# One more step of the decoder kernel: all expert rows summed on TensorE, and the expert ring worked two rows at a time

## The reference

```python
eidx = ...                      # 8 heads x 16 experts per token, by product keys and two top-16
g = jax.nn.softmax(fs, axis=-1)
u = u_tab[eidx]                 # (token, head, k, 1024)
v = v_tab[eidx]
a = jax.nn.gelu(jnp.einsum('pd,phkd->phk', xb, u), approximate=False)
return jnp.einsum('phk,phkd->pd', g * a, v)
```

## Time and profile before

| what | value |
|---|---|
| time, median of 3 runs | 2869.25 us (2858.16 to 2870.89) |
| profiled execution: span from first to last instruction | 2849.4 us |
| its own time beside the span | not listed; the three timed runs lie 9 to 21 us above this span |
| TensorE matmul busy | 1959.6 us, 69% |
| VectorE busy | 1637.4 us, 57% |
| ScalarE busy | 397.6 us, 14% |
| GpSimd busy | 652.7 us, 23% |
| mean granted TensorE clock | 0.786 of full speed |
| HBM traffic over the span | 240 GB/s |

### The profile page before, as it was taken

One profiled execution on the slowest core, in us unless ns is written; L12 is line 12 of the kernel. 1 busy time (PEld: TensorE's weight loads), 2 busy tenths in 40 slices (PEclk: granted clock), 3 DMA queues, 4 the chain that ended last, 5 costly groups with the idle time before them and its releaser, 6 DMA issues.

```text
span 2849.4 us, 19084 instructions
## 1 busy us (share of the span) xinstructions
PE 1959.6 (69%) x6466; PEld 1073.8 (38%) x6466; DVE 1637.4 (57%) x3431; ACT 397.6 (14%) x993; POOL 652.7 (23%) x585
## 2 busy tenths in 40 slices
PE   7997789997786522677777776775666676852334
PEld 4433556695486411333233333332233232631110
DVE  3303733302369887565666666655765666477766
ACT  1101123211011100111111011101121111010010
POOL 0000000000000213343344343332433342232232
PEclk9998755556997766789889888997888887676677
DMA  3214160003000457899989999896988889885586
GB/s 109 89 74 34 5 212 1 1 1 158 34 1 1 173 207 321 363 382 363 372 345 357 378 373 360 329 372 261 365 345 317 339 330 403 351 354 236 236 332 266
DMA packets 114049, 680.20 MB, mean 239 GB/s; under 512 B 28768, under 2 KB 32544, under 8 KB 36448
## 3 DMA queue, kind: packets, MB, share of 16 engines
q0 software_dynamic: 83168, 604.55, 53.6%
q1 hardware_dynamic: 30784, 74.44, 8.1%
HBM read 672.55 MB, written 10.55 MB: 240 GB/s over the span
## 4 chain that ended last, share of the span: by engine, by line
PE 35%; DMA 21%; DVE 19%; POOL 7%; issue 5%; ACT 2%; POOLq 0%; DVEq 0%; ACTq 0%
PE bank L696 31%; DMA arena<-in_uv,arena 21%; POOL arena L677 7%; DVE arena L1635 4%; PE bank L708 3%; DVE arena L1430 3%; DVE arena L1427 2%; PE bank L1733 2%; DVE arena L1432 1%; ACT arena L1309 1%; DVE arena L1652 1%; DVE arena L1472 1%; DVE arena L1473 1%; DVE arena L1469 1%; ACT arena L1107 1%
## 5 line engine op out<-in xcount | busy, mean ns | idle before, releaser
L696 PE MATMUL bank<-arena 128*128 128x512 f32 (+13 forms) x4672 | 1513.1, 487 | 783.6 <-ACT arena L1309 658.4
L696 PEld LDWEIGHTS bank<-arena 128*128 128x128 f32 (+4 forms) x4672 | 809.4, 224 | 1423.3 <-ACT arena L1309 703.3
L677 POOL DMA_INDIRECT arena<-in_uv,arena x544 | 616.7, 1134 | 1671.2 <-PE bank L696 1537.7
L1635 DVE CUSTOM_DVE_ANT_0 arena<-arena 128x1024 f32<-128x1024 f32 x544 | 655.4, 1225 | 440.2 <-DMA arena<-in_uv,arena 436.5
L1652 DVE SCALAR_TENSOR_TENSOR arena<-arena 128x1024 f32<-128x1024 f32 x267 | 343.2, 1285 | 9.5
L1733 PE MATMUL bank<-arena 128*128 128x512 f32 (+13 forms) x972 | 312.0, 481 | 46.1 <-DVE arena L2086 15.3
L1733 PEld LDWEIGHTS bank<-arena 128*128 128x128 f32 (+3 forms) x972 | 157.9, 197 | 199.6 <-issue 160.9
L708 PE MATMUL bank<-arena 128*128 128x128 f32 (+3 forms) x716 | 141.5, 342 | 36.1 <-DVE arena L1395 11.8
L1304 ACT ACTIVATE arena<-arena 128x4 f32<-128x4 f32 x136 | 27.7, 204 | 881.6 <-DVE arena L1635 877.6
L1107 ACT ACTIVATE arena<-bank 128x512 f32<-128x512 f32 (+6 forms) x229 | 112.3, 517 | 231.4 <-PE bank L708 209.0
L708 PEld LDWEIGHTS bank<-arena 128*128 128x128 f32 (+3 forms) x716 | 97.2, 172 | 122.2 <-issue 73.5
(11 more groups left out here) (219 smaller groups left out, 683.4 us busy)
## 6 DMA issues: line engine op xcount, KB each, us to landing
arena<-in_w_pq SPq DMA_DIRECT2D x8, 2048.0 KB, 12.8
arena<-in_w_in SPq DMA_DIRECT2D x6, 2048.0 KB, 7.6
arena<-in_uv,arena POOLq DMA_INDIRECT x544, 11.0
arena<-in_w SPq DMA_DIRECT2D x4, 2048.0 KB, 13.8
arena<-in_w_out SPq DMA_DIRECT2D x4, 2048.0 KB
arena<-in_xT SPq DMA_DIRECT2D x1, 2176.0 KB, 8.5
arena<-in_C SPq DMA_DIRECT2D x1, 2064.0 KB, 10.3
out_s_C<-arena SPq DMA_DIRECT2D x1, 2064.0 KB
```

Of the source, the lines that this page charges most:

```text
L677: nc.gpsimd.indirect_dma_start(uv[r], None, i["uv"], bass.IndirectOffsetOnAxis(eidx_u[:, t, s0 + r:s0 + r + 1], 0))\
L696: return te.matmul(out, l, r, start=start, stop=stop)
L1635: last = ve.tensor_tensor_reduce(out=uv[r][:, 0:D], in0=uv[r][:, 0:D], in1=x_sb[:, t, :], scale=1.0, scalar=0.0, op0=ALU.mult, op1=ALU.add ...
```

## The change

All eight rows of an iteration go through the diagonal matmul on TensorE. `acc_v`, its additions on VectorE, the matmul with the identity at a tile's end and the counters `s_vf` and `s_y` are gone. Dots, gelu, gate product, diagonals and the release of ring places go by pairs of rows instead of halves of four: VectorE makes two dots, then waits for the gelu of that pair and multiplies two gates; `s_free` counts four times an iteration, and GpSimd waits for it before every second gather. Ahead of the pieces VectorE now makes two dots of the next iteration, not four.

```diff
@@ GpSimd, gathers
                 for r in range(NR):
-                    if j and r % 4 == 0:
-                        pool.wait_ge(s_free, 2 * (j - 1) + r // 4 + 1)
-                    if j and r % 4 == 2:
-                        pool.wait_ge(s_vf, 2 * (j - 1) + r // 4 + 1)
+                    if j and r % 2 == 0:
+                        pool.wait_ge(s_free, 4 * (j - 1) + r // 2 + 1)
@@ TensorE
-                for r in (0, 1, 4, 5):
-                    n += 1
-                    pe_eng.wait_ge(s_dg, 4 * j + n)
+                for r in range(NR):
+                    pe_eng.wait_ge(s_dg, NR * j + r + 1)
                     for c2 in range(2):
                         last = mm(PB[c2][0:M, :], diag[r][:, 0:M], uv[r][:, D + c2 * 512:D + c2 * 512 + 512],
-                                  s0 + r == 0, False)
-                    if r % 4 == 1:
+                                  s0 + r == 0, s0 + r == GATHERS[t] - 1)
+                    if r % 2:
                         last.then_inc(s_free, 1)
-                if s0 == GATHERS[t] - NR:
-                    pe_eng.wait_ge(s_vf, 2 * (j + 1))
-                    for c2 in range(2):
-                        last = mm(PB[c2][0:M, :], (ident if t < PT else C("ident4"))[:, 0:M],
-                                  acc_v[:, c2 * 512:c2 * 512 + 512], False, True)
-                    last.then_inc(s_y, 1)
@@ ScalarE
-                for half in range(2):
-                    h4 = slice(4 * half, 4 * half + 4)
-                    act.wait_ge(s_dot, 2 * j + half + 1)
-                    sc.activation(gel[:, h4], dots[:, h4], ACT.Gelu).then_inc(s_gl, 1)
-                    act.wait_ge(s_w8, 2 * j + half + 1)
+                for pair in range(NR // 2):
+                    n, r = NR // 2 * j + pair, 2 * pair
+                    act.wait_ge(s_dot, n + 1)
+                    sc.activation(gel[:, r:r + 2], dots[:, r:r + 2], ACT.Gelu).then_inc(s_gl, 1)
+                    act.wait_ge(s_w8, n + 1)
                     if j:
-                        act.wait_ge(s_free, 2 * (j - 1) + half + 1)
-                    for r in (4 * half, 4 * half + 1):
-                        sc.activation(diag[r][:, 0:M], idm, ACT.Copy, scale=w8[:, r:r + 1]).then_inc(s_dg, 1)
+                        act.wait_ge(s_free, n + 1 - NR // 2)
+                    for k in (r, r + 1):
+                        sc.activation(diag[k][:, 0:M], idm, ACT.Copy, scale=w8[:, k:k + 1]).then_inc(s_dg, 1)
@@ VectorE, weigh_rows: the gate product of two rows is left, the additions go
-                for r in (4 * half + 2, 4 * half + 3):
-                    if s0 + r == 2:
-                        last = ve.tensor_scalar(acc_v, uv[r][:, D:2 * D], w8[:, r:r + 1], None, ALU.mult)
-                    else:
-                        last = ve.scalar_tensor_tensor(acc_v, uv[r][:, D:2 * D], w8[:, r:r + 1], acc_v,
-                                                       ALU.mult, ALU.add)
@@ VectorE, loop
             for j in range(N_IT):
                 weigh_rows(j, 0)
-                dot_rows(j, 1)
-                weigh_rows(j, 1)
+                for pair in range(1, NR // 2):
+                    dot_rows(j, pair)
+                    weigh_rows(j, pair)
                 if j + 1 in IT0[1:]:
                     t = IT0.index(j + 1) - 1
-                    dve.wait_ge(s_y, t + 1)
+                    dve.wait_ge(s_free, 4 * (j + 1))
                     layer_norm(norm_of(t), t, 1, P, PB).then_inc(s_fin, 1)
```

More of the change, by code:

```diff
@@ L482, in program @@
         s_free = sem("ring_quarters_multiplied")
-        s_vf = sem("ring_rows_added")
         s_uv = [sem(f"expert_rows_loaded{k}") for k in range(NR)]
@@ L488, in program @@
         s_dg = sem("diagonals_done")
-        s_y = sem("experts_summed")
         s_fin = sem("y_done")
@@ L1071, in iteration @@
                 M = ROWS[t]
-                n = 0
-                for r in (0, 1, 4, 5):
-                    n += 1
-                    pe_eng.wait_ge(s_dg, 4 * j + n)
+                for r in range(NR):
+                    pe_eng.wait_ge(s_dg, NR * j + r + 1)
                     for c2 in range(2):
                         last = mm(PB[c2][0:M, :], diag[r][:, 0:M], uv[r][:, D + c2 * 512:D + c2 * 512 + 512],
-                                  s0 + r == 0, False)
-                    if r % 4 == 1:
+                                  s0 + r == 0, s0 + r == GATHERS[t] - 1)
+                    if r % 2:
                         last.then_inc(s_free, 1)
-                if s0 == GATHERS[t] - NR:
-                    pe_eng.wait_ge(s_vf, 2 * (j + 1))
-                    for c2 in range(2):
-                        last = mm(PB[c2][0:M, :], (ident if t < PT else C("ident4"))[:, 0:M],
-                                  acc_v[:, c2 * 512:c2 * 512 + 512], False, True)
-                    last.then_inc(s_y, 1)
             pe_eng.wait_ge(s_qe, 4 * PT)
@@ L1628, in pieces, with dot_rows @@
                 yield from retrieve(PT)
-            def dot_rows(j, half):
+            def dot_rows(j, pair):
                 t = slots_of(j)[0]
-                for r in range(4 * half, 4 * half + 4):
+                for r in range(2 * pair, 2 * pair + 2):
                     dve.wait_ge(s_uv[r], 16 * (j + 1))
@@ L1638, in dot_rows, with weigh_rows @@
                 last.then_inc(s_dot, 1)
-            def weigh_rows(j, half):
+            def weigh_rows(j, pair):
                 t, s0 = slots_of(j)
-                h4 = slice(4 * half, 4 * half + 4)
-                dve.wait_ge(s_gl, 2 * j + half + 1)
-                ve.tensor_tensor(w8[:, h4], gel[:, h4], gw[:, t, s0 + 4 * half:s0 + 4 * half + 4], ALU.mult)\
+                r = 2 * pair
+                dve.wait_ge(s_gl, NR // 2 * j + pair + 1)
+                ve.tensor_tensor(w8[:, r:r + 2], gel[:, r:r + 2], gw[:, t, s0 + r:s0 + r + 2], ALU.mult)\
                   .then_inc(s_w8, 1)
                 settle(s_w8)
-                for r in (4 * half + 2, 4 * half + 3):
-                    if s0 + r == 2:
-                        last = ve.tensor_scalar(acc_v, uv[r][:, D:2 * D], w8[:, r:r + 1], None, ALU.mult)
-                    else:
-                        last = ve.scalar_tensor_tensor(acc_v, uv[r][:, D:2 * D], w8[:, r:r + 1], acc_v,
-                                                       ALU.mult, ALU.add)
[L1654 to L1658, removed]
             dve.wait_ge(s_sf, 4 * PT)
@@ L1676, in rest_vector @@
             for j in range(N_IT, N_IT + GATHERS[PT] // NR):
[L1677 to L1680, removed]
+                for pair in range(NR // 2):
+                    dot_rows(j, pair)
+                    weigh_rows(j, pair)
+            dve.wait_ge(s_free, 4 * (N_IT + GATHERS[PT] // NR))
             layer_norm(2 * PT + 1, PT, 1, NS, PB).then_inc(s_fin, 1)
```

## The result

The changed kernel takes 2753.0 us (median of 4 runs, 2744.0 to 2755.9) against 2863.7 us for the kernel before (4 runs). The ratio is 0.960, 95% interval 0.957 to 0.9635: 4.0% faster. I had predicted 2777 us, a gain of 92.5 us on the median of three runs then known.

The account below looks back on a forecast made before the run. The bound was taken to be a chain of waits round the ring-place loop, no single engine. Retrieval -53.5, compression 0, attention -25 and the end -14 sum to -92.5 us: from 2869.25 to 2777 us, range 2690 to 2865.

Parts of the forecast that it names:

- The chain, not VectorE's busy time, decides: Whole loop: VectorE's additions are 343 us of work but 1% of the chain; how the loop closes counts.
- Retrieval, row 1 in place of row 3: Iterations 0 to 4 and 57 to 61: VectorE's piece waits for row 1's landing, not row 3's; 53.5 us less.
- TensorE ends its ring at T+17 in such an iteration: Retrieval: even cold, TensorE ends its four pairs of rows 17 us after the first gates are ready (T).
- Compression, zero: Iterations 5 to 35: waiting for landings becomes waiting for TensorE at the same 25 us; change zero.
- The sum for a cycle of 3.9 iterations: Compression: TensorE's ring, pieces, transposes, output matmuls and waits over six pieces sum to 95.5 to 97.5 us.
- Attention, 25 us: Iterations 36 to 50: seven iterations gain 3.5 us each, 25 us less; the others stay.
- my seven iterations: Attention iterations 36, 37, 40, 43, 44, 45 and 50, where row 3's dot leads into VectorE's piece; 3.5 us gain each.
- The end, 14 us: Iterations 62 to 67, no pieces: transfers decide; 2 us for five iterations and 4 for two tile ends, 14 less.
- Rival 1: Compression and attention: TensorE becomes the bound, each of 46 iterations pays 2.4 us; +43, 2912 us; chance 0.13.
- Rival 2: Compression pays 1.5 us an iteration (46) and attention gains nothing: 2848 us; chance 0.19.
- Rival 3: Transfers become the bound in compression too, which gains 80 us: -172, 2697 us; chance 0.12.
- The rule weighed against the row: Compression: at about 358 GB/s, no iteration below 23.4 us; would lose some 12 us of gain, at the loop's end.

Follow-up runs that it names:

- the move alone: All rows on TensorE, but dots, gelu, gates and diagonals by four rows, four dots ahead, against the changed kernel: 2868.4 us, ratio 1.0007 to the kernel before.
- pairs alone: The changed kernel with rows 2, 3, 6 and 7 still added on VectorE: 2715.1 us, ratio 0.9475 to the kernel before.
- pair 1 on VectorE: The changed kernel with rows 2 and 3 of iterations 5 to 56 added on VectorE, ahead of the following dots: 2809.5 us, ratio 0.980.
- the version with pair 3 on VectorE: The changed kernel with rows 6 and 7 of iterations 5 to 56 added on VectorE: 2684.0 us, ratio 0.936 to the kernel before.
- with pair 3 there too: The changed kernel with rows 2, 3, 6 and 7 of iterations 5 to 56 added on VectorE: 2713.7 us, ratio 0.9455.

## Why the prediction held, step by step

The gain came within 3 us of the forecast between the profiled executions (95.3 against 92.5), and that is partly luck. Retrieval gave 5 us less than forecast, attention 5.5 less and the end 1 less; compression gave 15.6 where I had nothing. The time itself is 24 us below the forecast, of which 3 are this gain; the other 21 are there because I set it against a median that stood 20 us above the profiled span, while the median after stands 1 us below its own.

- **The chain, not VectorE's busy time, decides.** Right, and shown for the change as a whole: the move alone gives 1.0007, pairs alone 0.9475. Single additions do count where they stand ahead of dots (pair 1 on VectorE).
- **Retrieval, row 1 in place of row 3.** Right. I took 5.35 us for each of ten iterations, and they gave 4.8 (48.3 us in all). The dot of row 1 starts at T+16.1 (I had T+16.8). Four dots ahead put 43 of the 48 us back.
- **TensorE ends its ring at T+17 in such an iteration.** It ended at T+16.5.
- **Compression, zero.** The sum for a cycle of 3.9 iterations was 95.5 to 97.5 us against 98 before; measured are 762.2/31 x 3.9 = 95.9. So 0.5 to 2.5 us a cycle, 4 to 20 in all, stood in my own sum as gain, and I had rounded them to nothing; 15.6 came. By the runs it is a balance: the move with halves costs 13 us here, the finer pairs give 27 and two dots ahead 2. The picture behind it, a TensorE that is the bound at the same 25 us, was right in the chain and in busy share (93%), but it doesn't carry over to a price: of work removed from TensorE only a quarter to three fifths came back.
- **Attention, 25 us.** 19.5, but not from where I had put it. Of my seven iterations 37, 40, 44 and 45 gained 7.5, 4.6, 2.9 and 4.3 us, and 36, 43 and 50 lost 0.7, 2.5 and 4.0: 12.1 us together, half of the 24.5. The other 7 us came from the eight that I took for unchanged: 41 and 48, with two pieces each, lost 5.4 and 5.6, and the other six gained 18 between them. The total is near for the wrong reason. That two dots ahead of the piece are what gains here is right: four ahead put 24 us back.
- **The end, 14 us.** 13.0. At the very end, where nothing but gathers is left, the dots follow each other every 2.4 to 2.6 us, as the sum with 2.55 us a gather has it. In iterations 62 to 66, the finer pairs alone (four dots ahead, against halves) give 14 us, and going on to two ahead takes 1.6 back.
- **Rival 1 (TensorE the bound everywhere, slower)** didn't come. The clock rose to 0.99, as I had held against it, and even with halves compression lost 13 us, 0.4 an iteration, not 2.4. **Rival 2 (small gain)** wanted compression to lose 1.5 us an iteration; it gained 0.5. **Rival 3 (transfers the bound in compression)** didn't come with this change, but the version with pair 3 on VectorE is just that: 704 us and 403 GB/s. The obstacle that I gave, two long pieces behind a ring of 13.8 us, went when the ring got one pair shorter, with the pieces as they were.
- The rule weighed against the row, some 358 GB/s from HBM to a core (the Trainium skill, "SBUF — State Buffer", section "A bandwidth-pool intuition that's wrong"), is no ceiling here: 403 GB/s over 704 us. The eight gathers of an iteration alone, 8.39 MB in 22.7 us, are 369 GB/s, and the iteration is below the 23.4 us that I had drawn from the rule. The 12 us that I would have taken off for it follow from no sum in the prediction.

## What to carry to other kernels

In a ring that is refilled as it is used, find the loop from a place freed to the same place freed again, and shorten the step that it waits for (smaller groups, fewer items ahead of other work on an in-order queue, a release for each group) before taking work off any engine. Do it at every wait of the loop: here smaller groups gave 45 us, fewer dots ahead 65 more, and giving up the release by pairs lost 70. And when an engine becomes nearly full, take work from the place behind the last arrival, not from where the engine would wait anyway: the same 3.44 us gained 58 us of compression there and lost 29 where it was pair 1's, or 9 with the additions placed later.

## What the runs showed of the hardware

The granted clock went with the pauses in TensorE's work. In compression it stood at 0.98 to 0.99 with all rows on TensorE, in pairs or halves, and at 0.97 to 0.98 with pair 3 on VectorE. With pair 1 on VectorE and its additions ahead of pair 2's dots, which puts a pause behind pair 0, it was 0.92 (0.89 with pair 3 there too). The same 1600 instructions were 617.5 us of busy time at 0.98 and 651.2 us at 0.92. After one such pause of 4.69 us, 16 instructions took 9.39 us instead of 7.1, at a granted clock of 0.76. So less matmul work in the same loop made each instruction dearer here: 0.407 us of busy time each against 0.386 with all rows on TensorE.

Transfers that were mostly gathers of 8 KB rows kept 403 GB/s over 704 us, with a share of 0.98 of the DMA engines.
